# Second attention's maximum: relative bias added by GpSimd into the masks, head by head, instead of by TensorE products with the identity

## What is computed

```
s_idx = jnp.where(causal[None], s_idx, -jnp.inf)
_, sel = lax.top_k(s_idx, k_top)
...
lg_s = jnp.einsum('bqhc,bqkc->bqhk', ql, c_sel).astype(jnp.float32) * scale
bs = rel_bias[t5_bucket(q_pos[None, :, None] - sel)]
lg_s = lg_s + jnp.moveaxis(bs, -1, 2).astype(jnp.float32)
lg_s = jnp.where(valid[:, :, None, :], lg_s, -jnp.inf)
...
p = jax.nn.softmax(jnp.concatenate([lg_m, lg_s], axis=-1), axis=-1).astype(c.dtype)
```

## Time and profile before

| | |
|---|---|
| median of three runs | 3484.93 us |
| the profiled execution, its own time | 3490.18 us |
| its span | 3488.5 us |
| PE busy over the span | 3204.5 us (92%) |
| DVE busy over the span | 2204.1 us (63%) |
| ACT busy over the span | 1430.3 us (41%) |
| POOL busy over the span | 891.0 us (26%) |
| mean clock granted to TensorE | 0.964 of full |

### The profile page before, as it was taken

How to read it: one execution, slowest core, us unless ns; L and a number is a source line. 1 busy time by engine, 2 the same in 40 slices (tenths; PEclk the granted TensorE clock), 3 DMA queues, 4 the chain that set the end, 5 groups by cost and what they waited for, 6 DMA issues and landing times. The chain is left out here.

```text
span 3488.5 us, 43492 instructions
## 1 busy us (share of the span) xinstructions
PE 3204.5 (92%) x15136; PEld 2453.3 (70%) x15136; DVE 2204.1 (63%) x4308; ACT 1430.3 (41%) x2487; POOL 891.0 (26%) x817
## 2 busy tenths in 40 slices
PE   4999999899999998988789999997897899999898
PEld 4799888666666666866567887886775666666577
DVE  7111111267777776322389999995774799998766
ACT  5000001044444445212258999342555344444454
POOL 0111111257655460000421333344222111211000
PEclk9999999899999999999899999998999899999899
DMA  5321223485565533445311335364233623422354
GB/s 211 106 81 63 80 89 121 121 165 138 124 144 119 116 76 116 145 133 217 78 43 44 101 109 176 109 170 154 84 119 111 178 61 78 88 62 55 125 152 132
DMA packets 331916, 400.80 MB, mean 115 GB/s; under 512 B 100324, under 2 KB 249188, under 8 KB 319124
## 3 DMA queue, kind: packets, MB, share of 16 engines
q1 hardware_dynamic: 261080, 303.96, 30.7%
q10 hardware_dynamic: 66784, 73.17, 7.1%
q0 software_dynamic: 3840, 20.98, 2.6%
HBM read 265.39 MB, written 132.62 MB: 114 GB/s over the span
## 5 line engine op out<-in xcount | busy, mean ns | idle before, releaser
L2268 PE MATMUL f_pO<-f_PT,f_vv 128*128 128x512 f32 (+3 forms) x944 | 375.3, 479 | 0.0
L2291 ACT ACTIVATE f_PT<-f_pS 128x512 f32<-128x512 f32 (+3 forms) x472 | 223.1, 473 | 333.0 <-PE f_pS L2236 153.7
L2939 DVE TENSOR_SCALAR_CACHE_REDUCE sharedI<-xI,TI 128x768 bf16<-128x768 f32 (+10 forms) x276 | 339.6, 1296 | 5.4 <-DVE TI L2945 5.2
L2743 PE MATMUL cbank<-hT_high,cw_hi 128*128 128x512 f32 x800 | 320.0, 400 | 18.7 <-DVE cw_lo L2898 6.8
L585 PE MATMUL p_bank<-hT_high,p_w_hi 128*128 128x512 f32 (+1 forms) x768 | 304.8, 397 | 16.1 <-DVE p_w_lo L708 16.1
L2743 PE MATMUL cbank<-hT_high,cw_lo 128*128 128x512 f32 x800 | 316.7, 396 | 0.0
L2743 PE MATMUL cbank<-hT_low,cw_hi 128*128 128x512 f32 x800 | 316.4, 396 | 0.0
L2291 ACT ACTIVATE n_PT<-n_pS 128x512 f32<-128x512 f32 (+4 forms) x352 | 177.4, 504 | 336.8 <-PE n_pS L2248 183.2
L2268 PE MATMUL n_pO<-n_PT,n_vv 128*128 128x512 f32 (+4 forms) x704 | 310.2, 522 | 0.0
L585 PE MATMUL p_bank<-hT_low,p_w_hi 128*128 128x512 f32 (+1 forms) x768 | 303.6, 395 | 0.0
L585 PE MATMUL p_bank<-hT_high,p_w_lo 128*128 128x512 f32 (+1 forms) x768 | 302.7, 394 | 0.0
(11 more groups left out here) (424 smaller groups left out, 7408.0 us busy)
## 6 DMA issues: line engine op xcount, KB each, us to landing
f_zz<-scratch_z ACTq DMA_DIRECT2D x128, 128.0 KB, 3.1
c_w_first<-in_w_in_dram SPq DMA_DIRECT2D x26, 512.0 KB, 4.5
cw_raw<-in_w_in_dram SPq DMA_DIRECT2D x25, 512.0 KB, 4.4
p_w_raw<-in_w_in_dram SPq DMA_DIRECT2D x22, 512.0 KB, 4.0
lent<-scratch_qkb POOLq DMA_DIRECT2D x40, 256.0 KB, 10.2
scratch_z<-p_stage ACTq DMA_DIRECT2D x32, 256.0 KB, 2.4
scratch_qk_high<-p_stage ACTq DMA_DIRECT2D x32, 256.0 KB, 2.6
scratch_qk_low<-p_stage_low ACTq DMA_DIRECT2D x32, 256.0 KB, 3.2
```

The source lines that it names most:

```text
L2268: pe.matmul(pO[:, B % 2, c0:c1], lhsT=vv[0:nk, b, kt, :], rhs=PT[0:nk, u % PR, c0:c1], start=(kt == 0 and not heads[h].local), stop=(heads ...
L2291: act.activation(PT[0:nk, u % PR, c0:c1], pS[0:nk, u % SR, c0:c1], ACT.Exp, scale=0.125).then_inc(s_ex, 1)
L2743: last = pe.matmul(bank[:, p % RING, 0:wd], lhsT=w_part[pw][b][:, c, :], rhs=rhs, start=(c == 0 and a == 0), stop=(c == DC - 1 and a == 2))
L2939: own_.up(v.tensor_scalar(junk_v[:, own_.at % 2, 0:(i + 1) * P], scores(i), T[:, j:j + 1], None, compare, ALU.add, accum_out=count[:, j:j ...
```

## The change

The product with the identity that added the bias to the maximum's scores (line 2199) is gone. In its place GpSimd adds the bias into the mask `n_chosen` itself. Since the mask lies in SBUF for all heads, it adds for head h the difference between head h's bias and head h-1's, both rounded to bf16 (`change`), tile by tile: 16 additions a head, of 240 columns (144 in tile 0), 128 in all. Each waits until the maximum of head h-1 for this tile has been taken, and each is followed by a wait for its own end. DVE's `take_max` waits for the tile's addition where the chunk touches the band. `n_bias` keeps only the two parts that the sum needs.

```
@@ stage_attend, tiles @@
-            bias = m.sb(n_("bias"), [P, 2, 3, BAND], F32R)
+            bias = m.sb(n_("bias"), [P, 2, 2, BAND], F32R)
+            band, change = m.sb(n_("band"), [P, 2, BAND], BF16), m.sb(n_("change"), [P, BAND])
@@ gpsimd, split_bias @@
-                gp.tensor_copy(bias[:, b, 0:2], biasf[:, b]).then_inc(s_bias, 1)
+                step(gp.tensor_copy(band[:, b], biasf[:, b, 0]))
+                if h == 0:
+                    step(gp.tensor_copy(change[:], band[:, b]))
+                else:
+                    step(gp.tensor_tensor(change[:], band[:, b], band[:, 1 - b], ALU.subtract))
+                gp.tensor_copy(bias[:, b, 0], biasf[:, b, 1]).then_inc(s_bias, 1)
                 gp.wait_ge(s_bias, 2 * h + 1)
-                gp.tensor_tensor(bias[:, b, 2], biasf[:, b, 1], bias[:, b, 1].bitcast(F32), ALU.subtract).then_inc(s_bias, 1)
+                gp.tensor_tensor(bias[:, b, 1], biasf[:, b, 1], bias[:, b, 0].bitcast(F32), ALU.subtract).then_inc(s_bias, 1)
                 gp.wait_ge(s_bias, 2 * h + 2)
+
+            def bias_into_masks(h, i):
+
+                first = max(i * P - BACK, 0)
+                seen = sw.seen(i)
+                at = OFF[i] + i * NMETA
+                if h == 0:
+                    gp.wait_ge(s_mk[i // 4], 64)
+                else:
+                    gp.wait_ge(s_mx, 1 + max(n for n, (g, j, r, c) in enumerate(sw.chunks) if (g, 4 * j + r) == (h - 1, i)))
+                gp.tensor_tensor(chosen[:, at + first:at + seen], chosen[:, at + first:at + seen],
+                                 change[:, first - i * P + BACK:], ALU.add).then_inc(s_band, 1)
+                gp.wait_ge(s_band, NT * h + i + 1)
@@ gpsimd, order @@
                 split_bias(h)
                 if h >= 1:
                     split_queries(h)
-                if h == 0:
-                    ones_beside_values(0)
-                    for b in range(1, NB):
-                        blank(b)
-                        ones_beside_values(b)
+                for i in range(NT):
+                    bias_into_masks(h, i)
+                    if h == 0 and i == 3:
+                        ones_beside_values(0)
+                        for b in range(1, NB):
+                            blank(b)
+                            ones_beside_values(b)
@@ tensor, max_scores @@
-                    if rel is not None:
-                        pe.wait_ge(s_bias, 2 * h + 1)
...
-                if rel is not None and near(i, c, wd):
-                    to, frm, k = near(i, c, wd)
-                    last = pe.matmul(pM[:, n % 2, to:to + k], lhsT=ident_r[:], rhs=bias[:, b, 0, frm:frm + k],
-                                     start=False, stop=True, skip_group_check=True)
                 last.then_inc(s_max, 1)
@@ tensor, scores @@
-                        for z in (1, 2):
+                        for z in range(2):
@@ vector, take_max @@
+                    if near(i, c, wd):
+                        v.wait_ge(s_band, NT * h + i + 1)
```

More of the change, by code:

```diff
@@ L1865, in stage_attend @@
             s_masked = m.sem(n_("probabilities_masked"))
+            s_band = m.sem(n_("bias_in_masks"))
         s_rq, s_part = m.sem(n_("raw_queries_loaded")), m.sem(n_("head_split"))
```

## The result

The changed kernel takes 3509.26 us (median of five runs, 3504.52 to 3516.95) against 3484.93 (3484.16 to 3490.28): a ratio of 1.0066, 95% interval 1.0054 to 1.0077, or 19 to 27 us more. The forecast was 3514. One execution of a later run (all additions inside the split) took 3699.26 us at a granted clock of 0.832 throughout and is left out of that run's ratio.

What follows compares the result with a forecast made beforehand. DVE was taken to end one part of each head and PE another. The terms, -9 + 21 - 9 + 21.6 + 4, gave +28 or 29 us on the median 3484.9: 3514 us, range 3491 to 3545.

Steps and rivals of the forecast that it cites:

- term 5: Heads 0 and 1: additions delay head 0's fills and fifth addition, with slight contention and waiting, +4 us in all.
- Term 1: 184 removed PE products save about 0.11 us each, only where PE ends the work: -9 us, bounds 0 and 50.
- ten products a head: Of a head's 23 products, some 10 to 11 lie where PE fills the time and count, 0.11 us each.
- PE was the true bound: Rival: products cost their busy time, 50.2 us come back, additions barely touch DVE; -25 us, 3460; chance 6%.
- Terms 2 and 3: Heads 2 to 7: DVE's first maximum waits behind GpSimd's split, +21 us; maskings freed of contention give back 9.
- the whole stall is lost: Where DVE ends the work, PE works on for about one unit only, so all 3.1 us per stall count.
- Term 4: Sixteen GpSimd additions per head behind the split slow DVE's maskings: 3.6 us per head, six heads, +21.6 us.
- expected mean of 680 ns: Sign of being right: the masking's mean over the stage's 352 maskings rises from 633 ns to about 680.
- lower price: By the skill page's cycle accounting, a 240-column addition takes 0.52 us, not 0.71; the sum would be some 4 us lower.
- two-input work alone: GpSimd's two-input subtractions slow DVE's two-input SBUF maskings, 0.69 to 1.57 us; beside one-input casts they take 0.96.

Runs made afterwards that it cites:

- wait alone: Kernel before, plus DVE's first maximum of heads 1 to 7 waiting for the end of GpSimd's query split; products kept, no additions: ratio 1.0073.
- additions alone: Kernel before, plus sixteen GpSimd additions per head (heads 1 to 7) into a tile nobody reads; products kept, DVE waits for none: ratio 1.0023.
- late split alone: Kernel before with only the rest of each head's query split held until 35 of the previous head's 44 units are scored: ratio 0.9989.
- products alone gone: Kernel before without the 184 bias products of the maximum and nothing in their place: ratio 0.9988.
- wait filled: The wait alone kernel plus 24 idle TensorE products in heads 2 to 7 where PE would stand; ratio 1.0052 to the kernel before.

## Why the prediction came out, by its terms

**The account.** The parts alone make -4 (products) + 25 (wait) + 8 (additions of heads 1 to 7) + 2 (head 0, term 5 below) = +31; together they made +24. Some of the additions run while DVE stands still or waits for PE, where they cost nothing, which may be the difference; the intervals allow none at all.

**Term 1, -9.** Measured -4 (-9 to 0). The start-to-start distance was the right price and not the busy time: 50 us of busy time brought 4. That ten products a head count fully was too much by the middle of the interval; its end, 9 us, and the 0.7 us a head of the profile leave room for most of them. The rival "PE was the true bound" is refuted by this one run.

**Terms 2 and 3, +21 and -9.** The stalls sum to 23.5 us, forecast 21, none in head 1, as said. Which head has the long one was wrong: 5.54 us came in head 7 and 4.32 in heads 3 and 4, not 5.5 in head 6 (which by the term's own steps, 5.86 - 0.4 + 0.43 + 0.15, should read 6.0); where DVE stands when the split begins drifts from head to head. The relief of the maskings was right (11 for 9). But the pair was worth +25, not +12. The step that failed is "the whole stall is lost" as an upper limit: behind each stall, in most heads, PE goes on at a lower granted clock, and DVE waits 2.1 to 2.5 us for it (wait alone). With PE kept busy the clock stays up and the waits shrink to 0.54 us a head; that a standing PE has nothing done ahead may be what is left of them. The run with idle products brings back 7 of these 13 us, some of it perhaps by its shorter stalls and its fewer low stretches elsewhere; the rest is not split further.

**Term 4, +21.6.** Measured +8 (5 to 11). The number and duration of the additions were right (0.75 us each, 13.1 us for 16; forecast 0.85 and 15.5). The mis-sized quantity is the masking beside them, 0.80 and not 1.57 us (and 1.57 is the mean of three in head 2; all 20 beside the split's subtractions in the kernel before have 1.47). The subtractions of the split looked nearest in kind, but they were twice as long, and length decides. In the changed kernel's own trace 31 such maskings take 0.81 and 11 that lie wholly beside subtractions 1.47. The expected mean of 680 ns, measured 621, fails for this reason. The stage's maskings add up: 222.7 + 8.2 (additions alone) - 11.3 (wait alone) = 219.6, against 218.3. The lower price that the prediction works out for additions of 0.52 us is 6 us off the sum by the term's own rate (0.19 x 16 x 0.34 x 6), not 4; nothing hangs on it.

**Term 5, +4.** The delay in head 0 came as forecast. DVE waits for the fifth addition, which stands behind the fills:

```profile
2710.75 0.69 DVE L2394 CUSTOM_DVE_ANT_0 n_junk<-n_pM,n_chosen 128x512 bf16<-128x512 f32 x1 [7.91 <-POOL n_chosen L2087]
```

Before, it waited 5.80 us there for the mask. From head 0's first maximum to its first masking it is 20.5 us instead of 18.5, and so in all four kernels that have additions in head 0, and in none of the others (18.1 to 18.9). It does not show in the time, because from its first masking to that of head 1 the first head came out 4.5 us shorter. This is no gain of the change: the kernels with the wait alone and with the late split alone show 3 and 5 us of it too, and the stretch at the low clock in which head 0 begins lasted 44.4 us before, 41.0 after and 37.5 with the wait alone; where it lasted 44.4 us again (products alone gone, wait filled) the first head was shorter by at most 1 us. It varies with when the clock comes up.

**The sum.** Terms 2 and 3 were 13 too low and term 4 was 14 too high; term 1 promised 5 too much, and of term 5's 4 us the 2 of head 0 are in the trace. The forecast was right on the sign, the place and the length of the stall, and right in total partly by luck.

**Open.** Why the stalls differ by 1.2 us from head to head was not tried, nor why one in six is followed by no drop in the clock. In the changed kernel that is head 5: around its stall DVE's maskings fall 3.0 us further behind those of the kernel before, around the others 3.9 to 5.3.

## What to carry to other kernels

When an operation moves to an idle engine, look at what stands ahead of it in that engine's queue: here the change cost nothing that could be measured at two of three places in the queue, and some 24 us at the third. Price a stall of the bounding engine at its length plus what the engines behind it must catch up, which here was 16 us on 20 by the account of the run with the wait alone. And the price of contention is read only from neighbours of the same length, not only of the same kind.

## What the hardware showed that was not expected

A DVE instruction with two inputs in SBUF is held by a two-input GpSimd instruction for a time that follows the length of GpSimd's instruction: 512 columns cost the masking 0.8 us, 240 columns 0.1 to 0.3, 60 columns nothing. At 512 columns that is half of one GpSimd instruction (1.55 us). Casts do it too, which the prediction put down to two-input work alone: beside the split's casts, one input, 512 columns, 0.61 us each, 14 maskings of the kernel before take 0.92 us on average. The maximum, with one input in PSUM, is not held (0.67). The Trainium skill (GPSIMD Engine Reference, "Specifications") has this contention between the two engines; the runs agree, and add that cutting GpSimd's work into short instructions makes it nearly free for DVE's instruction: the first 14 of 60 columns cost GpSimd 0.53 us each where 512 cost 1.55, 2.9 times as much per column, and over the whole head 32.7 us where instructions of 512 columns took 12.4. What that does to the time of the kernel was not measured.

A standstill of PE of 2.41 us with the wait alone, and of 3.12 in the changed kernel, in a stage where it was 94% busy, was followed by a granted clock of 0.72 over the next 6 us; behind one stall in six, of 3.73 us with the wait alone, it was not.
